# Two more up units per layer with seven products, two plain ones fewer, and the first unit's preparation reordered

## The chip, the cores and the metric

One core of one Trainium2 chip runs the whole program in one launch. The metric is the device time in microseconds (us). Engines: TensorE (PE, with its weight loads PEld), VectorE (DVE), ScalarE (ACT), GpSimd (POOL), and SyncE (SP), which issues the loads of the weights.

## The reference, cut to what matters

A decoder trunk of two layers over 512 tokens of width 1024, all in float32. Each layer is a token mixer, a cross-attention and a gated MLP, each between two RMS norms. The change is in the MLP's up projection:

```
def conv_ffn(h, w_up, conv_w, conv_b, w_down):
    u = h @ w_up                      # (512, 1024) @ (1024, 5632)
    a, b = u[..., :D_FF], u[..., D_FF:]        # D_FF = 2816
    a = causal_depthwise_conv(a, conv_w, width 3) + conv_b
    return (gelu(a) * b) @ w_down
```

## The kernel before, in words

**Products of three.** Every float32 operand is split into a high and a low fp32r part, and a product is three matmuls (`three`, L2161 to L2165): low by high, high by low, high by high. The high part of a weight is a copy by ACT, the low part a subtraction by POOL.

**Units.** The weights come in 70 units per layer of at most 1 MB, through a ring of two buffers `raw`, `w_hi` and `w_lo` (even units in slot 0, odd ones in slot 1). Units 36 to 57 are the up projection: for each of 11 pairs a unit of 256 value columns (even) and one of 256 gate columns (odd). SP loads a unit once the unit two before it has been turned into its low parts.

**Plain units.** A plain unit of the up projection is 2 column tiles x 8 blocks of k x 3 = 48 matmuls of 512 columns (`cols_gemm`). Units 36 and 37 do the same by halves of the tokens, as 256-column matmuls, in buffers of their own (`up_hi`, `up_lo`). The last plain unit has a loop of its own, with k outermost, which gives its places in the ring back in four steps (`part_spent`).

**Units with seven products.** From `U_SEVEN` on, `SEVENS` units are computed by the Winograd form of Strassen's scheme. Tokens (2 x 256), k (2 x 512) and columns (2 x 128) are cut in two each, and seven products of half-sized blocks take the place of eight: 7 x 4 x 3 = 84 matmuls of 256 columns. In the order in which PE issues them, with the bank that they add to: "11" (c11), "s2" (c21), "s1" (c12), "12" (c11), "s3" (c21), "s4" (c12), and "22" (c21), which `product_4` issues behind the "11" of the next unit. Within a unit:

- On the weights' side DVE makes four sums `s1`, `s2`, `s3`, `s4` (`part_sum`). `s2` and the unit's quarter 21 stand in upper halves of PSUM banks, where ACT copies the quarter (`copy_21`, place `psum_21`). ACT makes the high parts (`part_high`, order `HI_PARTS`: 11, s1, s2, 12, s4, s3), POOL the low parts (`part_low`, order `LO_PARTS`: 11, s1, 12, s3, s4), and DVE that of s2 (`part_s2_low`). The low part of s1 overwrites the sum s1, so POOL waits with it until s2 is made.
- The parts lie in eight places of the ring (`place_of`, `HELD`); `wait_place` waits until the place's last user is done.
- Between products, ACT copies c11 after "11" (`keep_first`, signal `kept_1`), DVE adds it to c21 and c12 (`keep_sixth`, `keep_fifth`), and `make_22`, `make_12`, `make_21` finish the four quarters. "12" may be issued only after `kept_1`, "s3" only after `kept_16`, "s4" only after `kept_15`.

**Token sums.** The tokens' side needs four sums of quarters of the activations, once per layer, `tok_sum[0..3]`, each with a high part (ACT, `token_high(i)`) and a low part. DVE makes sums 0, 1 and 3 (`token_sum`), POOL makes sum 2, the "third token sum" (`token_sum_3`, three passes), and its low part (`token_low_3`, needed by product "s3"). DVE makes the other low parts. `token_high(3)` and its low part write over a quarter of `a_hi` and `a_lo`, so they wait for the last plain unit. They are used by product "22".

**Behind the products** DVE does the convolution's taps (`conv_taps`) and the gating (`gate`), and ACT the gelu (`gelu_of`), for each column tile f of 22. For the plain pairs f = 0 to 5, for the others f = 6 to 21, whose first tap ACT does (`tap`).

**Order.** Every engine executes one list written out by hand, in order; only semaphores tie them together. The lists around the start of the seven-product units are in the ACT block (from `token_high(0)`), the DVE block (from `token_sum(0)`), the POOL block (the loop over u) and the PE block (behind the loop over units 36 and 37).

Of the kernel before, what the change touches and what calls it, by code (L numbers as in the profile page):

```python
# [48 lines left out]
UNITS = 70  # L49


U_SEVEN, SEVENS = 42, 16
PLAIN = 3
HELD = 8
assert UNITS % RING == 0
IN_W = [512] * 5 + [280]
# [207 lines left out]
def build(nc, x, mem, positions, norm_mix_pre, norm_mix_post, w_in, w_out, cmp_pe_k, cmp_pe_v,  # L264
# [4 lines left out]
    with ctx:  # L269
# [369 lines left out]

        def psum_21(w):  # L640

            return banks[:, 1024 * (2 * (w % 2) if w else 3):][:, 0:1024].rearrange("p (i n) -> p i n", i=2)[:, :, 256:512]

        def psum_s2(w):

# [261 lines left out]
        def _(pool):  # L907
# [26 lines left out]
            for l in range(DEPTH):  # L934
# [90 lines left out]
                    inc(pool.tensor_tensor(part_of(w_lo, w, "22"), quarter(U_SEVEN + w, 1, 1), part_of(w_hi, w, "22").bitcast(F32), ALU.subtract), part_22_lo)  # L1025

                for u in range(UNITS):
                    if u == U_SEVEN - 2:
                        token_sum_3()
                    if u == U_SEVEN:  # L1030
                        token_low_3()
                        for w in range(SEVENS):
                            part_low(w, "11")
                            if w:
                                part_22_low(w - 1)
                            for part in LO_PARTS[1:]:
                                part_low(w, part)
                        part_22_low(SEVENS - 1)
                    if U_SEVEN <= u < U_SEVEN + SEVENS:
                        continue  # L1040
                    if u == U_OUT + RING:
                        xk_rest()
                    if u == U_XO + 1:
                        for i in range(16):
                            xscale(i)
                    if u == U_XK:
                        for half in range(LO_STEPS.count(-1)):
                            low_half(U_XK, half)
                        for i in range(NI + 1):
                            if i == 0:  # L1050
                                pool.wait_ge(qk.sem, qk.at(l, 1))
                                inc(pool.memset(vc_tiles[:], 0.0), vc_cleared)
                            if i < NI and KIND[i] == "sb":
                                stick_relu(i)
                            if i + 1 < NI and KIND[i + 1] == "cmp":
                                cmp_shift(i + 1)
                            if i >= 2 and KIND[i - 2] == "cmp":
                                cmp_scale(i - 2)
                            if i and SOFT[i - 1]:
                                pool_scale(i - 1)  # L1060
                            if i and KIND[i - 1] == "sb":
                                stick_log(i - 1)
                            if i in O_LO_STEPS:
                                o_rest(O_LO_STEPS[i])
                            if i in LO_STEPS:
                                low_half(U_XK + LO_STEPS.index(i) // 2, LO_STEPS.index(i) % 2)
                    if U_XK <= u < U_OUT + RING:
                        continue
                    if l == 0 and u < 2:
                        pool.wait_ge(hi_made.sem, hi_made.at(0, 2 * u + 2))  # L1070
                        part_lo, part, part_hi = (v(u, 1) for v in (lo_half, raw_half, hi_half))
                        pool.tensor_tensor(part_lo[:, 0], part[:, 0], part_hi[:, 0].bitcast(F32), ALU.subtract).then_inc(pro_third, 1)
                        pool.wait_ge(pro_low, 2 + u)
                        inc(pool.tensor_tensor(part_lo[:, 1], part[:, 1], part_hi[:, 1].bitcast(F32), ALU.subtract), lo_made, 2)
                        continue
                    if u == in_unit(4, 1):
                        pool.wait_ge(first_low.sem, first_low.at(l, 1))
                        low_half(u, 1, 2)
                        continue
                    if u == U_UP + 1:  # L1080
                        pool.wait_ge(rows_done.sem, rows_done.at(l, T + 2))
                    for half in range(2):
                        low_half(u, half)
# [3 lines left out]
        def _(act):  # L1087
# [28 lines left out]
            for l in range(DEPTH):  # L1116
# [21 lines left out]
                def cast_to(n):  # L1138

                    cast_halves(2 * n)  # L1140
# [337 lines left out]
                def copy_21(w):  # L1478

                    u = U_SEVEN + w  # L1480
                    act.wait_ge(raw_landed[u % RING], landed(l, u))
                    if w == 0:
                        act.wait_ge(gT_done.sem, gT_done.at(l, 4))
                    elif w == 1:
                        act.wait_ge(gT_done.sem, gT_done.at(l, 6))
                    else:
                        done = (conved, gT_done)[w % 2]
                        act.wait_ge(done.sem, done.at(l, column(w - 2, 0) + 1))
                    inc(act.activation(k_of(psum_21(w)), by_halves(quarter(u, 0, 1)), ACT.Copy), copied_21)
# [9 lines left out]
                gelu_of(0)  # L1499
                token_high(1)  # L1500
                gelu_of(1)
                cast_to(U_UP + 5)
                token_high(2)
                gelu_of(2)
                gelu_of(3)
                cast_to(U_UP + 6)
                copy_21(0)
                for part in HI_PARTS[:4]:
                    part_high(0, part)
                gelu_of(4)  # L1510
                gelu_of(5)
                for part in HI_PARTS[4:]:
                    part_high(0, part)
                token_high(3)
                for w in range(SEVENS):
                    after_value, more = w % 2 == 1, w + 1 < SEVENS
                    if after_value:
                        tap(w - 1, 0)
                    keep_first(w)
                    part_high(w, "22")  # L1520
                    if more:
                        part_high(w + 1, "11")
                    if after_value:
                        tap(w - 1, 1)
                    elif w:
                        gelu_of(column(w - 1, 1))
                    if more:
                        copy_21(w + 1)
                        for part in ("s1", "s2", "12"):
                            part_high(w + 1, part)  # L1530
                    if after_value:
                        gelu_of(column(w, 0))
                    if more:
                        part_high(w + 1, "s4")
                        part_high(w + 1, "s3")
                    if w in (8, 10, 12):
                        g_parts((w - 8) // 2)
                gelu_of(NF - 1)
                cast_to(U_DOWN + 1)
                act.preload_act_table_set("natural_log_exp_and_others")  # L1540
# [22 lines left out]
        def _(dve):  # L1563
# [59 lines left out]
            for l in range(DEPTH):  # L1623
# [392 lines left out]
                def part_sum(w, part):  # L2016
# [8 lines left out]
                        ins = dve.tensor_tensor(by_halves(dst), by_halves(quarter(u, 1, 0)), k_of(psum_s2(w)), ALU.subtract)  # L2025
                    elif part == "s2":
                        dve.wait_ge(part_summed.sem, part_summed.at(l, nth(SUMS, w, "s1")))
                        if w >= 2 and w % 2 == 0:
                            dve.wait_ge(tapped.sem, tapped.at(l, w))
                        ins = dve.tensor_tensor(k_of(dst), by_halves(s1), by_halves(quarter(u, 0, 0)), ALU.subtract)  # L2030
# [48 lines left out]
                conv_taps(1)  # L2079
                gate(0)  # L2080
                gate(1)
                token_sum(3)
                token_low(0)
                conv_taps(2)
                token_low(1)
                conv_taps(3)
                gate(2)
                gate(3)
                conv_taps(4)
                part_sum(0, "s1")  # L2090
                part_sum(0, "s2")
                conv_taps(5)
                part_sum(0, "s3")
                part_sum(0, "s4")
                part_s2_low(0)
                gate(4)
                gate(5)
                for w in range(SEVENS):
                    if w:
                        make_12(w - 1)  # L2100
                        columns(w - 1, 0)
                        if w in (10, 12, 14):
                            g_rest((w - 10) // 2)
                        make_21(w - 1)
                    if w == 0:
                        dve.wait_ge(tok_hi_made.sem, tok_hi_made.at(l, 4))
# [44 lines left out]
        def _(pe):  # L2151
# [28 lines left out]
            for l in range(DEPTH):  # L2180
# [557 lines left out]
                                inc(ins, (up_psum, unit_used)[m])  # L2738

                cols_gemm(U_UP + 2, up_bank(1, 0), up_psum)  # L2740
                cols_gemm(U_UP + 3, up_bank(1, 1), up_psum)
                pe.wait_ge(gT_done.sem, gT_done.at(l, 2))
                cols_gemm(U_UP + 4, up_bank(2, 0), up_psum)
                hi, lo = unit(U_SEVEN - 1)
                for k in range(KD):
                    if k == 4:
                        rest(U_SEVEN - 1)
                    for m in range(2):
                        mm = slice(P * m, P * m + P)
                        ins = three(bank(up_bank(2, 1) + m), hi[:, k, mm], lo[:, k, mm], a_hi[:, k, :], a_lo[:, k, :], k == 0, k == KD - 1)  # L2750
                        if k == KD - 1:
                            inc(ins, (up_psum, unit_used)[m])
                    if k in (1, 3, 5):
# [18 lines left out]
                def wait_banks(w, name):  # L2772

                    if w < 2:
                        done, n = (conved, gT_done)[w], {"c11": 5, "c12": 6, "c21": 3}[name]
                    else:
                        done, n = (conved, gT_done)[w % 2], column(w - 2, name == "c21") + 1
                    pe.wait_ge(done.sem, done.at(l, n))
# [64 lines left out]
```

## Time and profile before

| | us |
|---|---|
| median of 3 runs (1657.83 to 1657.98) | 1657.86 |
| the profiled execution's own time | 1657.59 |
| its span, first to last instruction | 1655.9 |
| PE busy in the span | 1642.2 (99%) |
| DVE / ACT / POOL busy | 838.5 / 846.6 / 968.3 |
| mean granted TensorE clock | 0.999 |

Times in rows are microseconds from the start of the span. The columns of the stretch in the last group are PE, PEld, DVE, ACT, POOL, granted clock, DMA share and GB/s. In a timeline the first number is the start, the second the duration, behind them the engine, line, operation, output<-inputs, shape and count. An idle time before it, if there is any, is in brackets with what ended it. Durations of matmuls overlap: their pace is read from start to start. The first layer's up projection lies from 477 to 708 us.

### The profile page before, as it was taken

The page shows a single profiled execution, that of the slowest core. Times are in us where ns is not written, and L with a number is a line of the kernel's source. Part 1 is how long each engine was busy: PE and PEld are TensorE (multiplying, and loading weights), DVE is VectorE, ACT ScalarE, POOL GpSimd, SP SyncE. Part 2 cuts the span into 40 slices and gives each one's busy share as a digit, 9 for nine tenths or more (in the row PEclk, how much of TensorE's full clock was granted, in tenths as well). Part 3 has the DMA queues.
Part 4 walks back from the last instruction along what each step waited for, and adds up shares of the span by engine and source line. Part 5 has one row for each costly group of instructions (what it writes and reads, how often), then busy time and mean ns, then how long its engine had stood idle before and what let it go on. Part 6 is the DMA issues. An engine that isn't in the chain of part 4 may idle for free.

```text
span 1655.9 us, 26967 instructions
## 1 busy us (share of the span) xinstructions
PE 1642.2 (99%) x10369; PEld 1401.6 (85%) x10369; DVE 838.5 (51%) x1733; ACT 846.6 (51%) x1650; POOL 968.3 (58%) x689
## 2 busy tenths in 40 slices
PE   9999999999999999999999999999999999999998
PEld 7888766888888999988888887768888989999886
DVE  3454676072368677721243456652532877777113
ACT  6326777263463566532362367763643636566222
POOL 4456668464338777755624467674634387776552
PEclk9999999999999999999999999999999999999999
DMA  6224111143123233332323340112422223332421
GB/s 231 77 94 142 52 27 52 64 141 102 64 77 102 77 103 103 103 127 102 112 94 94 101 142 27 27 52 89 141 76 68 81 94 102 103 103 83 139 85 76
DMA packets 101210, 154.39 MB, mean 93 GB/s; under 512 B 4396, under 2 KB 76380, under 8 KB 101084
## 3 DMA queue, kind: packets, MB, share of 16 engines
q1 hardware_dynamic: 98572, 147.16, 27.3%
q10 hardware_dynamic: 2512, 5.51, 1.0%
q8 instruction: 84, 1.38, 0.4%
q14 instruction: 42, 0.34, 0.1%
HBM read 150.56 MB, written 2.10 MB: 92 GB/s over the span
## 4 chain that ended last, share of the span: by engine, by line
PE 95%; ACT 1%; issue 1%; DVE 1%; POOL 1%; DVEq 0%; ACTq 0%; POOLq 0%
PE banks L2163 27%; PE banks L2165 26%; PE banks L2164 26%; PE banks L2478 4%; PE banks L2531 4%; PE banks L2507 4%; PE banks L2291 1%; PE banks L2207 1%; DVE proj L1851 1%; PE banks L2527 0%; PE banks L2675 0%; PE banks L2195 0%; POOL w_lo L938 0%; ACT w_hi L1135 0%; ACT rows L1098 0%
## 5 line engine op out<-in xcount | busy, mean ns | idle before, releaser
L938 POOL TENSOR_TENSOR w_lo<-raw,w_hi 128x1024 fp32r<-128x1024 f32 (+2 forms) x198 | 486.2, 2475 | 422.6 <-ACT w_hi L1135 409.8
L1135 ACT ACTIVATE w_hi<-raw 128x1024 fp32r<-128x1024 f32 (+2 forms) x200 | 195.5, 1020 | 328.9 <-PE banks L2165 321.2
L2163 PE MATMUL banks<-w_hi,a_lo 128*128 128x512 f32 (+1 forms) x864 | 332.5, 385 | 0.1
L2165 PE MATMUL banks<-w_hi,a_hi 128*128 128x512 f32 (+1 forms) x864 | 330.1, 382 | 0.0
L2164 PE MATMUL banks<-w_lo,a_hi 128*128 128x512 f32 (+1 forms) x864 | 330.0, 382 | 0.0
L2163 PE MATMUL banks<-a_hi,w_lo 128*128 128x256 f32 (+1 forms) x768 | 245.2, 319 | 0.0
L2165 PE MATMUL banks<-a_hi,w_hi 128*128 128x256 f32 (+1 forms) x768 | 244.6, 318 | 0.0
L2164 PE MATMUL banks<-a_lo,w_hi 128*128 128x256 f32 (+1 forms) x768 | 244.5, 318 | 0.0
L2163 PEld LDWEIGHTS banks<-w_hi,a_lo 128*128 128x128 f32 x864 | 162.3, 188 | 32.8 <-issue 1.7
L2165 PEld LDWEIGHTS banks<-w_hi,a_hi 128*128 128x128 f32 x864 | 162.2, 188 | 31.5
L2164 PEld LDWEIGHTS banks<-w_lo,a_hi 128*128 128x128 f32 x864 | 162.3, 188 | 30.3
L2165 PEld LDWEIGHTS banks<-a_hi,w_hi 128*128 128x128 f32 x768 | 146.4, 191 | 10.1
L2164 PEld LDWEIGHTS banks<-a_lo,w_hi 128*128 128x128 f32 x768 | 146.4, 191 | 9.7
L2163 PEld LDWEIGHTS banks<-a_hi,w_lo 128*128 128x128 f32 x768 | 146.2, 190 | 9.5
L1020 POOL TENSOR_TENSOR w_lo<-w_sum,w_hi 128x512 fp32r<-128x512 f32 x64 | 83.0, 1296 | 56.5 <-DVE banks L2030 40.9
L2164 PE MATMUL banks<-tok_lo,w_hi 128*128 128x256 f32 x384 | 108.8, 283 | 0.0
L2163 PE MATMUL banks<-tok_hi,w_lo 128*128 128x256 f32 x384 | 108.7, 283 | 0.0
L2165 PE MATMUL banks<-tok_hi,w_hi 128*128 128x256 f32 x384 | 108.3, 282 | 0.0
L1962 DVE TENSOR_TENSOR a_lo<-gT,a_hi 128x1024 fp32r<-128x1024 f32 x18 | 28.7, 1593 | 153.7 <-ACT a_hi L1435 153.7
L1020 POOL TENSOR_TENSOR w_lo<-raw,w_hi 128x512 fp32r<-128x512 f32 x64 | 84.8, 1324 | 25.9 <-ACT w_hi L1468 25.9
L1837 DVE CUSTOM_DVE_ANT_0 banks<-banks,causal 128x128 f32<-128x128 f32 (+3 forms) x160 | 75.6, 512 | 40.2 <-PE banks L2478 40.2
L948 POOL TENSOR_SCALAR proj<-proj,rden,gates 128x128 f32<-128x128 f32 (+3 forms) x128 | 76.4, 609 | 22.9 <-DVE rden L1855 22.5
(321 smaller groups left out, 3461.8 us busy)
## 6 DMA issues: line engine op xcount, KB each, us to landing
raw<-in_ffn_w_up SPq DMA_DIRECT2D x44, 1024.0 KB, 5.1
raw<-in_ffn_w_down SPq DMA_DIRECT2D x20, 1024.0 KB, 4.8
raw<-in_w_in SPq DMA_DIRECT2D x19, 1024.0 KB, 5.0
raw<-in_x_wk SPq DMA_DIRECT2D x8, 1024.0 KB, 5.5
raw<-in_x_wv SPq DMA_DIRECT2D x8, 1024.0 KB, 4.9
raw<-in_x_wq SPq DMA_DIRECT2D x8, 1024.0 KB, 5.2
raw<-in_x_wo SPq DMA_DIRECT2D x8, 1024.0 KB, 4.9
raw<-in_cmp_wk SPq DMA_DIRECT2D x4, 1024.0 KB, 5.2
```

The source lines that it names most:

```text
L938: inc(pool.tensor_tensor(lo_half(u, half), raw_half(u, half), hi_half(u, half).bitcast(F32), ALU.subtract), lo_made, n)
L948: inc(pool.tensor_scalar(p, p, r, gate_of(i, hp), ALU.mult, ALU.mult), scaled_pool)
L1020: inc(pool.tensor_tensor(lo, src, hi.bitcast(F32), ALU.subtract), piece_lo)
L1135: inc(act.activation(hi_half(u, half), raw_half(u, half), ACT.Copy), hi_made)
L1837: inc(dve.tensor_tensor_reduce(x, x, causal[:, S - n:S], -1.0, 3.0e38, ALU.add, ALU.min, stat(neg_max, i, hp)), maxed)
L1962: inc(dve.tensor_tensor(part_lo, gT[:, k[0]:k[-1] + 1, :], part_hi.bitcast(F32), ALU.subtract), g_lo)
L2163: pe.matmul(dst, st_lo, mv_hi, start=first, stop=False, skip_group_check=shared)
L2164: pe.matmul(dst, st_hi, mv_lo, start=False, stop=False, skip_group_check=shared)
L2165: return pe.matmul(dst, st_hi, mv_hi, start=False, stop=last, skip_group_check=shared)
L2478: ins = pe.matmul(s_bank(i, hp, n + extra, key_at(i) - extra), qT[half, m, P * t:P * t + P], keys(row, n, extra)[half], start=True, stop=True)
L2507: ins = pe.transpose(bank(4 + hp, P, P * k), probs(i, hp)[:, P * k:P * k + P], ident[:])
L2531: ins = pe.matmul(bank(6, P, P * t)[half], proj[:, k, col:col + HD], pT(i)[:, kg, P * k:P * k + P], start=kind != "win" and t == 0 and k = ...
```

## The change

`PLAIN` goes from 3 pairs to 2, `U_SEVEN` from 42 to 40 and `SEVENS` from 16 to 18. So in each layer units 40 and 41 are computed with seven products; units 36 to 39 stay plain, and 39 takes over the loop that frees its places step by step. The lists of ACT and DVE around the start are rearranged. In POOL's list the third token sum stands where it stood, behind the low halves of unit 39; what stood behind it (the low halves of units 40 and 41) is gone, and the low part of the third sum moves from ahead of the first unit's parts to between its "12" and its "s3". Quarter 21 of the first unit goes to banks 4 and 5 in place of 6 and 7. The steps that make the first parts of the down projection's input keep their distance from the end.

```
-U_SEVEN, SEVENS = 42, 16
-PLAIN = 3
+U_SEVEN, SEVENS = 40, 18
+PLAIN = 2
 def psum_21(w):
-    banks[:, 1024 * (2 * (w % 2) if w else 3):] ...
+    banks[:, 1024 * (2 * (w % 2) if w else 2):] ...
# POOL
-    if u == U_SEVEN - 2:
+    if u == U_SEVEN:
         token_sum_3()
-    if u == U_SEVEN:
-        token_low_3()
         for w in range(SEVENS):
             part_low(w, "11")
             if w:
                 part_22_low(w - 1)
             for part in LO_PARTS[1:]:
+                if w == 0 and part == "s3":
+                    token_low_3()
                 part_low(w, part)
# ACT, copy_21
-    if w == 0:
-        act.wait_ge(gT_done.sem, gT_done.at(l, 4))
-    elif w == 1:
-        act.wait_ge(gT_done.sem, gT_done.at(l, 6))
+    if w < 2:
+        act.wait_ge(gT_done.sem, gT_done.at(l, 2))
# ACT, list
 gelu_of(1)
-cast_to(U_UP + 5)
 token_high(2)
+copy_21(0)
+for part in HI_PARTS[:2]:
+    part_high(0, part)
 gelu_of(2)
+for part in HI_PARTS[2:4]:
+    part_high(0, part)
 gelu_of(3)
-cast_to(U_UP + 6)
-copy_21(0)
-for part in HI_PARTS[:4]:
-    part_high(0, part)
-gelu_of(4)
-gelu_of(5)
 for part in HI_PARTS[4:]:
     part_high(0, part)
 token_high(3)
...
-    if w in (8, 10, 12):
-        g_parts((w - 8) // 2)
+    if w in (10, 12, 14):
+        g_parts((w - 10) // 2)
# DVE, part_sum "s2"
+    if w == 0:
+        dve.wait_ge(conved.sem, conved.at(l, 4))
# DVE, list
 gate(0)
 gate(1)
-token_sum(3)
 token_low(0)
+token_low(1)
+part_sum(0, "s1")
 conv_taps(2)
-token_low(1)
 conv_taps(3)
-gate(2)
-gate(3)
-conv_taps(4)
-part_sum(0, "s1")
 part_sum(0, "s2")
-conv_taps(5)
 part_sum(0, "s3")
 part_sum(0, "s4")
 part_s2_low(0)
-gate(4)
-gate(5)
+token_sum(3)
+gate(2)
+gate(3)
 for w in range(SEVENS):
...
-    if w in (10, 12, 14):
-        g_rest((w - 10) // 2)
+    if w in (12, 14, 16):
+        g_rest((w - 12) // 2)
# PE
 cols_gemm(U_UP + 2, up_bank(1, 0), up_psum)
-cols_gemm(U_UP + 3, up_bank(1, 1), up_psum)
-pe.wait_ge(gT_done.sem, gT_done.at(l, 2))
-cols_gemm(U_UP + 4, up_bank(2, 0), up_psum)
 ...                        # the loop of unit U_SEVEN - 1, now into up_bank(1, 1)
-    if w < 2: done, n = (conved, gT_done)[w], {"c11": 5, "c12": 6, "c21": 3}[name]
+    if w < 2: done, n = (conved, gT_done)[w], {"c11": 1, "c12": 2, "c21": 3}[name]
```

## Rows read from the trace of the kernel before

**Rows 1.** Part 1 of the page: busy time of each engine.

```profile
PE 1642.2 (99%) x10369; PEld 1401.6 (85%) x10369; DVE 838.5 (51%) x1733; ACT 846.6 (51%) x1650; POOL 968.3 (58%) x689
```

**Rows 2.** Waits of PE over the span: us in total, times, longest.

```profile
PE banks L2163 <- ACT xkT L1318: 3.8, 4, 1.0
PE banks L2155 <- POOL ident L915: 2.5, 1, 2.5
```

**Rows 3.** PE's timeline: unit 38's first matmul, then first ones of products.

```profile
503.34 0.40 PE L2163 MATMUL banks<-a_hi,w_lo 128*128 128x512 f32 x1
...
546.87 0.28 PE L2163 MATMUL banks<-a_hi,w_lo 128*128 128x256 f32 x1
...
567.02 0.28 PE L2163 MATMUL banks<-a_hi,w_lo 128*128 128x256 f32 x1
```

**Rows 4.** POOL's timeline from 507 us, the end of the plain units.

```profile
507.90 3.38 POOL L997 TENSOR_TENSOR tok_sum<-a_hi 128x1024 f32<-128x1024 f32 x1
511.24 2.40 POOL L998 TENSOR_TENSOR tok_spare<-a_lo 128x1024 f32<-128x1024 f32 x1
513.72 3.27 POOL L1000 TENSOR_TENSOR tok_sum<-tok_sum,tok_spare 128x1024 f32<-128x1024 f32 x1
...
533.49 2.40 POOL L1005 TENSOR_TENSOR tok_lo<-tok_sum,tok_hi 128x1024 fp32r<-128x1024 f32 x1
...
538.72 1.29 POOL L1020 TENSOR_TENSOR w_lo<-w_sum,w_hi 128x512 fp32r<-128x512 f32 x1
...
551.25 1.30 POOL L1025 TENSOR_TENSOR w_lo<-raw,w_hi 128x512 fp32r<-128x512 f32 x1
```

**Rows 5.** DVE's timeline in the same stretch, and one row of the second layer.

```profile
512.04 0.69 DVE L1969 TENSOR_TENSOR gT<-gel,banks 128x512 f32<-128x512 f32 x1 [0.20 <-ACT gel L1442]
512.65 2.08 DVE L2008 TENSOR_TENSOR tok_sum<-a_hi,tok_sum 128x1024 f32<-128x1024 f32 x1
514.76 3.31 DVE L2009 TENSOR_TENSOR tok_sum<-tok_sum,a_lo 128x1024 f32<-128x1024 f32 x1
...
523.55 1.22 DVE L2014 TENSOR_TENSOR tok_lo<-tok_sum,tok_hi 128x1024 fp32r<-128x1024 f32 x1
...
537.52 0.74 DVE L1985 TENSOR_SCALAR conv<-banks,vecs 128x512 f32<-128x512 f32 x1
...
539.75 0.68 DVE L2035 TENSOR_TENSOR w_sum<-raw,banks 128x512 f32<-128x512 f32 x1
540.35 0.68 DVE L2025 TENSOR_TENSOR s_sum<-raw,banks 128x512 f32<-128x512 f32 x1
...
553.03 0.68 DVE L2035 TENSOR_TENSOR w_sum<-raw,banks 128x512 f32<-128x512 f32 x1
...
1333.65 2.08 DVE L2008 TENSOR_TENSOR tok_sum<-a_hi,tok_sum 128x1024 f32<-128x1024 f32 x1
```

**Rows 6.** ACT's timeline in the same stretch.

```profile
517.02 1.06 ACT L1453 ACTIVATE tok_hi<-tok_sum 128x1024 fp32r<-128x1024 f32 x1 [0.52 <-POOL tok_sum L1000]
...
529.56 0.58 ACT L1489 ACTIVATE banks<-raw 128x512 f32<-128x512 f32 x1
...
536.91 0.63 ACT L1468 ACTIVATE w_hi<-w_sum 128x512 fp32r<-128x512 f32 x1
...
547.13 1.06 ACT L1453 ACTIVATE a_hi<-tok_sum 128x1024 fp32r<-128x1024 f32 x1 [4.29 <-PE banks L2165]
548.50 0.38 ACT L1476 ACTIVATE keep<-banks 128x256 f32<-128x256 f32 x1 [0.31 <-PE banks L2165]
...
557.43 1.15 ACT L1468 ACTIVATE w_hi<-raw 128x512 fp32r<-128x512 f32 x2
```

**Rows 7.** SP's timeline and its DMAs' time to landing: the load of unit 44.

```profile
552.63 0.37 SPq L889 DMA_DIRECT2D raw<-in_ffn_w_up  x1
...
DMA to landing us min/median/max: 5.0/5.1/5.3
```

**Rows 8.** A stretch of the steady seven-product units: its length, then busy time of each engine.

```profile
568.00:690.00 122.00, 122.00 (x1019) 122.00 (x1018) 89.22 (x159) 76.37 (x138) 92.46 (x74) 1.00 0.32 105
```

More of the change, by code:

```diff
@@ L640, in psum_21 @@
         def psum_21(w):
-            return banks[:, 1024 * (2 * (w % 2) if w else 3):][:, 0:1024].rearrange("p (i n) -> p i n", i=2)[:, :, 256:512]
+            return banks[:, 1024 * (2 * (w % 2) if w else 2):][:, 0:1024].rearrange("p (i n) -> p i n", i=2)[:, :, 256:512]
         def psum_s2(w):
@@ L2749, in _ @@
                         mm = slice(P * m, P * m + P)
-                        ins = three(bank(up_bank(2, 1) + m), hi[:, k, mm], lo[:, k, mm], a_hi[:, k, :], a_lo[:, k, :], k == 0, k == KD - 1)
+                        ins = three(bank(up_bank(1, 1) + m), hi[:, k, mm], lo[:, k, mm], a_hi[:, k, :], a_lo[:, k, :], k == 0, k == KD - 1)
                         if k == KD - 1:
@@ L2774, in wait_banks @@
                     if w < 2:
-                        done, n = (conved, gT_done)[w], {"c11": 5, "c12": 6, "c21": 3}[name]
+                        done, n = (conved, gT_done)[w], {"c11": 1, "c12": 2, "c21": 3}[name]
                     else:
```

## The prediction

> **What bounds the kernel.** I read the page's busy times first: PE is busy for 1642.2 of 1655.9 us, the next engine, POOL, for 968.3 [rows 1]. The reader should see that only two things can move the time: the number and width of PE's matmuls, and holes in PE's stream. The list of PE's waits says how few holes there are: 6.3 us in the whole span, and none in the up projection [rows 2]. So the change is worth what it takes off PE's stream, less the holes that it tears. PE's timeline gives the price of either kind of unit [rows 3], and the timelines of POOL, DVE and ACT between 507 and 558 us [rows 4 to 6] give what is needed to lay the new lists out by hand. The second layer shows the same at 821.0 us later (DVE's L2008 of 2.08 us at 512.65 comes again at 1333.65 [rows 5]), so one layer is worked out and counted twice.
>
> **What PE saves.** From 503.34 to 546.87 lie the 192 matmuls of the four plain units 38 to 41, back to back: 43.53 / 4 = 10.88 us a unit. From 546.87 to 567.02 lie 14 products: 1.44 us each, 10.08 us for the seven of a unit [rows 3]. So one conversion saves 0.80 us, not the eighth that the count of columns promises (1.36), because a 256-column matmul takes 120 ns, more than half of the 227 ns of a 512-column one. Two units in two layers: 4 x 0.80 = **3.2 us saved** if PE never waits. That is 0.19% of the time.
>
> **What is late.** What prepares the first seven-product unit (w = 0) now has until the end of unit 39, at 503.34 + 2 x 10.88 = 525.1, where it had until 546.87. The two plain units that went away were the cover for the token sums. The steps up to `gate(1)` are untouched (DVE ends them at 512.7 [rows 5]). I lay out the rest:
>
> - POOL and DVE get in each other's way. POOL's L998 ends at 513.64; DVE's L2008, issued at 512.65, takes 2.08 where its like takes 1.22 alone (523.55), and ends at 514.73. POOL's L1000, issued at 513.72, then takes 3.27 instead of 2.40 and ends at 516.99; DVE's L2009, issued at 514.76, takes 3.31 and ends at 518.07 [rows 4, 5]. So they take turns: about 1.1 us for DVE, 2.26 for POOL, and whoever waits goes next. A DVE operation with a PSUM input doesn't take part (0.68 to 0.75 us).
> - DVE's `token_low(0)` and `token_low(1)` are operations of the same shape in the place of those two, so they end at 514.7 and 518.07. ACT's `token_high(2)` still starts at 517.02, behind POOL's third sum, and ends at 518.08 [rows 6]; `copy_21(0)` now stands behind it and ends at 518.56 (0.58).
> - DVE: s1 518.66 to 519.34, the taps of f = 2 and 3 (3 x 0.78 each, after 537.52 [rows 5]) to 523.8, s2 to 524.5, s3 to 525.1 (each 0.68 or a little more). PE's "11" waits for s3 and starts at about 525.2: a hole of 0.1 us. ACT makes the high part of s2 by 525.17, of "12" by 525.69; DVE makes s4 by 525.93 and the low part of s2 by 526.54, just in time for "s2" at 526.64.
> - POOL can make the low part of s1 only after s2: 524.6 to 525.9 (1.29 [rows 4]); that of "12" 525.9 to 527.15; and then, newly in this place, `token_low_3`.
> - DVE comes to `token_sum(3)` at 526.45, two SBUF passes. The first waits for POOL's "12" and runs 527.15 to 528.25. POOL's `token_low_3`, waiting since 527.15, takes 528.25 to 530.5. The second pass depends on the first and so cannot have got in ahead of it; it runs 530.5 to 531.6.
> - ACT stands in `token_high(3)` until then: 531.65 to 532.7 (1.06). Queued behind it is `keep_first(0)`, 532.6 to 533.0 (0.38 [rows 6]). That copy of c11 was free to go since 526.7, but PE's "12", due at 525.2 + 3 x 1.44 = 529.5, waits for it. **Hole: 3.5 us.** In the kernel before, `token_high(3)` began at 547.13 and the copy was made at 548.9, against a "12" due at 551.2.
> - Behind that, "s3" is due at 534.5 and needs `keep_sixth(0)`, which stands in DVE's list behind `gate(2)`, `gate(3)` and the low part of token sum 3. These gates end at 532.8; POOL ends the low part of s3 in the same 0.1 us. If DVE goes first, `keep_sixth` is done at 534.3: no hole. If POOL does, 1.1 us later: a hole of 1.05.
> - The next units inherit lateness. s3 of w = 1, which had 1.8 us in hand (made at 553.71, product due at 555.50 [rows 5]), is made at 537.6 against 537.4 (another 0.2, or 0.4 in POOL's case). SP loads unit w = 2 once POOL has the low part "22" of w = 0, which came 2.9 us ahead of the second unit's first product (552.55 [rows 4]; the issue is at 552.63, landing takes 5.1 [rows 7]) and now comes 0.5 behind it. ACT's copy of the new unit, the second operation at 557.43, had just 0.1 to 0.3 us in hand [rows 6], so it slips by 3.3 us; s3 of w = 2 had 2.0 in hand and costs perhaps 0.25. After that the preparation catches up, since DVE and POOL are idle for a quarter of the steady stretch (89.22 and 92.46 of 122 us busy [rows 8]).
>
> Sum of a layer: 0.1 + 3.5 + 0 + 0.2 + 0.25 = 4.05 if DVE wins the tie, 0.1 + 3.5 + 1.05 + 0.4 = 5.05 if POOL does. Neither order is favoured by a row, so I take the middle, **4.5 us a layer**, 9.0 for two. Net 9.0 - 3.2 = +5.8.
>
> **What is taken at nothing.** The added unit's work on DVE, ACT and POOL lies under its 10.08 us of PE, as in the steady stretch, where no engine but PE is busy for more than 76% [rows 8]. The end of the up projection moves as a whole: g_parts, g_rest and the cast of unit 58 keep their distance to the last product; cover gone, each would open a hole of its own in the down projection. The wait on `conved` 4 is on DVE's own last operation, 0.04 us. The other bank of quarter 21 changes nothing in length.
>
> **A rule beside the turns.** The rows show POOL and DVE taking turns by whole instructions, 3.3 us for a pair [rows 4, 5]. The Trainium skill (SBUF — State Buffer, Who interferes with whom) says that DVE with two SBUF inputs and GpSimd exclude each other for a whole instruction, and that the order of issue decides; by that, the trace agrees. It speaks against this change: it puts `token_sum(3)` and `token_low_3` at one moment, with ACT and PE behind the loser. Without the rule, with both at full speed, the hole would be 0.7 us.
>
> **Rivals.**
>
> 1. *No turns.* `token_sum(3)` finds the port free or wins both times: 526.45 to 528.75, the copy of c11 at 530.15, a hole of 0.7. A layer costs 0.1 + 0.7 + at most 0.2: 1.0. Net 2.0 - 3.2 = -1.2: 1656.7. For it: the margins are tenths (POOL's "12" would have to be over by 526.45, not 527.15). Against it: three collisions in a row went the other way.
> 2. *No hole at all.* Faster: all steps run 0.8 us earlier than I lay them, for instance if POOL's third sum, which now sees the same two collisions, ended early. It decides from `kept_1` at 529.5, and then gives the whole 3.2: 1654.7, which at 0.19% is still just inside of no change. The other side of 0.2% needs 0.1 us more than the arithmetic has.
> 3. *Late weights.* The load of w = 2 and then of w = 3 slips more than the next units catch up. If ACT's 3.3 us are not absorbed, because `keep_fifth` stands behind the s1 of the next unit, each of the next two units opens about 1 us: 6.5 us a layer, net +9.8: 1667.7. For it: 0.1 us in hand at 557.97. Against it: the next load has 1.6 us in hand again.
> 4. *The clock.* The granted clock is 1.0 wherever PE waits in this trace, but no wait is over 1.0 us behind the start [rows 2]. If a hole of 3.5 us took it from 2.4 to 1.2 GHz, each product at that level would take 1.44 us more; two of them in each layer give +5.8: 1669.5. The Trainium skill (TensorE: Matmul & The Clock Gate, What's actually happening) describes such a fall after idling; no row here shows it.
>
> **How the numbers follow.** Chances: my forecast 0.50, rival 1 0.20, rival 2 0.10, rival 3 0.13, rival 4 0.07. The time: 1657.86 + 5.8 = **1663.7** (the profiled execution, at 1657.59, would come to 1663.4). 0.2%, about what a measurement of this kernel can tell from no change, is 3.3 us, so the limits are 1654.5 and 1661.2. Slower: the forecast, 3 and 4, less the part of the forecast in which a hole is a microsecond shorter: 0.64. Within 0.2%: rivals 1 and 2 and that part: 0.32. Faster by more: 0.04. The range leaves out rival 4, half of rival 2 and the far end of 3: **1655.5 to 1667.0**. The forecast's own range is 1662.8 to 1664.8.
>
> **What would show it.** Units 38 and 39 at 10.88 us, w = 0 starting at about 525.2. In PE's waits, a new one of 3.5 us, twice, on ACT's `keep_first` (the operation keep<-banks), with `token_high(3)` right ahead of it on ACT and DVE's tok_sum<-tok_sum,a_lo, 3.3 us long, ahead of that. Perhaps 1 us on keep<-banks,keep of DVE. Steady units of 10.08 us from w = 3 on. I am wrong if DVE's two passes for the fourth token sum take 1.2 us each, if "12" starts before 531, or if the clock drops below 1.0 there.

## The result, and the profile after

| | before | changed |
|---|---|---|
| median of 4 runs, us | 1657.86 | 1667.36 |
| lowest to highest | 1657.83 to 1657.98 | 1666.39 to 1668.57 |
| ratio, with its 95% interval | | 1.0058 (1.0040 to 1.0075) |
| the profiled execution: its time, its span | 1657.59, 1655.9 | 1668.25, 1666.5 |

The changed kernel is slower by 9.5 us, 0.57%. Slower was forecast, by 5.8; the time lies 0.36 us above the stated range. The four runs come in two pairs, 1666.39 and 1666.46, which lie inside the range, and 1668.25 and 1668.57; the profile is of the run of 1668.25. Part 1 of the page of the changed kernel, against [rows 1]: PE has 144 matmuls more (336 of 256 columns in place of 192 of 512) and gains 2.8 us of busy time in a span that is 10.6 longer.

```profile
PE 1645.0 (99%) x10513; PEld 1410.9 (85%) x10513; DVE 859.0 (52%) x1769; ACT 859.6 (52%) x1682; POOL 982.1 (59%) x705
```

The list of PE's waits in the changed kernel, which answers to [rows 2], names the forecast hole: twice, on ACT's `keep_first` (L1476), 3.3 us each. (The list counts from the end of the matmul before; counted by how much later than due the product starts, as the prediction does, it is 3.5.) Two short ones are new as well.

```profile
PE banks L2157 <- ACT keep L1476: 6.7, 2, 3.3
PE banks L2157 <- ACT xkT L1318: 3.9, 4, 1.0
PE banks L2149 <- POOL ident L915: 2.5, 1, 2.5
PE banks L2157 <- issue: 0.5, 1, 0.5
PE banks L2157 <- DVE w_sum L2033: 0.4, 1, 0.4
```

PE's timeline of the changed kernel in the first layer, against [rows 3]: unit 38's first matmul, the first of "11", of "12" and of "s3" of the first seven-product unit.

```profile
503.43 0.40 PE L2157 MATMUL banks<-a_hi,w_lo 128*128 128x512 f32 x1
...
525.79 0.35 PE L2157 MATMUL banks<-a_hi,w_lo 128*128 128x256 f32 x1 [0.41 <-DVE w_sum L2033]
...
533.68 0.42 PE L2157 MATMUL banks<-a_hi,w_lo 128*128 128x256 f32 x1 [3.34 <-ACT keep L1476]
...
536.24 0.41 PE L2157 MATMUL banks<-tok_hi,w_lo 128*128 128x256 f32 x1
```

From "12" to "s3" pass 2.56 us where a product takes 1.44. What lies in there is seen in the stretches of the same kernel (columns as in [rows 8]; the last but two is the granted clock), in the first layer and in the second.

```profile
528.00:530.00 2.00, 2.00 (x19) 2.00 (x18) 1.97 (x2) 0.00 (x0) 2.00 (x1) 1.00 0.00 0
530.00:532.00 2.00, 0.34 (x3) 0.14 (x2) 2.00 (x1) 0.00 (x0) 2.00 (x2) 1.00 0.00 0
532.00:534.00 2.00, 0.32 (x2) 0.35 (x3) 2.00 (x4) 1.80 (x4) 2.00 (x2) 0.96 0.00 0
534.00:536.00 2.00, 2.00 (x11) 2.00 (x11) 2.00 (x3) 1.06 (x3) 1.89 (x2) 0.50 0.00 0
536.00:538.00 2.00, 2.00 (x15) 2.00 (x14) 2.00 (x3) 0.63 (x1) 2.00 (x2) 0.69 0.00 0
...
1360.00:1362.00 2.00, 1.46 (x7) 1.20 (x7) 2.00 (x5) 0.53 (x1) 2.00 (x2) 0.50 0.00 0
1362.00:1364.00 2.00, 2.00 (x11) 2.00 (x11) 2.00 (x2) 0.63 (x3) 1.30 (x2) 0.50 0.00 1
1364.00:1366.00 2.00, 2.00 (x12) 2.00 (x11) 1.65 (x4) 1.70 (x4) 2.00 (x2) 0.50 0.86 288
```

PE idles from 530.3 to 533.7, and behind that the clock is granted at half, 1.2 GHz, for 3 to 4 us in the first layer and for some 7 in the second. An engine that reads "busy 2.00 of 2.00" with 11 matmuls in place of 19 is the sign, since PE's starts are then 213 ns apart in place of 120 ("12" to "s3": 2.56 us for 12 matmuls).

DVE's timeline of the changed kernel, against [rows 5], shows the chain that makes the hole: `token_low` 0 and 1 (5.42 together), s2 (L2028) and s3 (L2033), the two passes of token sum 3, the gates, its low part (L2101) and `keep_sixth` (L2045).

```profile
512.74 5.42 DVE L2010 TENSOR_TENSOR tok_lo<-tok_sum,tok_hi 128x1024 fp32r<-128x1024 f32 x2
...
524.36 0.70 DVE L2028 TENSOR_TENSOR banks<-w_sum,raw 128x512 f32<-128x512 f32 x1 [0.46 <-DVE conv L1983]
524.97 0.68 DVE L2033 TENSOR_TENSOR w_sum<-raw,banks 128x512 f32<-128x512 f32 x1
...
526.93 1.92 DVE L2004 TENSOR_TENSOR tok_sum<-a_hi,tok_sum 128x1024 f32<-128x1024 f32 x1
528.88 3.29 DVE L2005 TENSOR_TENSOR tok_sum<-tok_sum,a_lo 128x1024 f32<-128x1024 f32 x1
532.09 1.27 DVE L1965 TENSOR_TENSOR gT<-gel,banks 128x512 f32<-128x512 f32 x2
533.29 2.33 DVE L2101 TENSOR_TENSOR a_lo<-tok_sum,a_hi 128x1024 fp32r<-128x1024 f32 x1
535.54 0.41 DVE L2045 TENSOR_TENSOR keep<-banks,keep 128x256 f32<-128x256 f32 x1
```

ACT's timeline, against [rows 6]: idle for 4.33 us in front of `token_high(3)`, with the copy of c11 queued behind it.

```profile
532.20 1.06 ACT L1453 ACTIVATE a_hi<-tok_sum 128x1024 fp32r<-128x1024 f32 x1 [4.33 <-DVE tok_sum L2005]
533.16 0.37 ACT L1476 ACTIVATE keep<-banks 128x256 f32<-128x256 f32 x1
```

POOL's timeline, against [rows 4]: the low part of "12", that of token sum 3 between DVE's two passes, that of s3 behind the second.

```profile
526.45 1.32 POOL L1020 TENSOR_TENSOR w_lo<-raw,w_hi 128x512 fp32r<-128x512 f32 x1
527.71 3.37 POOL L1005 TENSOR_TENSOR tok_lo<-tok_sum,tok_hi 128x1024 fp32r<-128x1024 f32 x1
531.05 2.25 POOL L1020 TENSOR_TENSOR w_lo<-w_sum,w_hi 128x512 fp32r<-128x512 f32 x1
```

**Where the 10.6 us of the profiled spans are.** From unit 38's first matmul to the first one of the down projection the kernel before took 204.80 us in either layer. The changed kernel took 208.90 and 210.47: less the 1.60 saved, holes and clock cost 5.70 and 7.27. Another 0.3 lies ahead of the two stretches, and 0.6 behind the second, where the last stores take 2.5 us to land in place of 2.0.

### The profile page after: what moved, and what is told of

Read it like the earlier page. It is cut to its first block, busy times and chain, and to the rows that moved or that the text cites. A ratio compares the mean times of both kernels' runs of the same rounds, so it can differ in the third digit from the quotient of the medians.

```text
span 1666.5 us, 27429 instructions
## 1 busy us (share of the span) xinstructions
PE 1645.0 (99%) x10513; PEld 1410.9 (85%) x10513; DVE 859.0 (52%) x1769; ACT 859.6 (52%) x1682; POOL 982.1 (59%) x705
## 4 chain that ended last, share of the span: by engine, by line
PE 91%; POOL 3%; DVE 2%; ACT 2%; issue 1%; DVEq 0%; ACTq 0%; POOLq 0%
PE banks L2157 25%; PE banks L2158 25%; PE banks L2159 25%; PE banks L2472 4%; PE banks L2525 4%; PE banks L2501 4%; POOL w_lo L938 2%; PE banks L2285 1%; PE banks L2201 1%; DVE proj L1847 1%; PE banks L2521 0%; PE banks L2669 0%; ACT w_hi L1135 0%; PE banks L2189 0%; POOL tok_sum L997 0%
## 5 line engine op out<-in xcount | busy, mean ns | idle before, releaser
L938 POOL TENSOR_TENSOR w_lo<-raw,w_hi 128x1024 fp32r<-128x1024 f32 (+2 forms) x190 | 463.6, 2459 | 412.3 <-ACT w_hi L1135 399.6
L1135 ACT ACTIVATE w_hi<-raw 128x1024 fp32r<-128x1024 f32 (+2 forms) x192 | 187.5, 1018 | 323.7 <-PE banks L2159 316.2
L2157 PE MATMUL banks<-a_hi,w_lo 128*128 128x256 f32 (+1 forms) x768 | 239.9, 312 | 7.1 <-ACT keep L1476 6.7
L2158 PE MATMUL banks<-a_lo,w_hi 128*128 128x256 f32 (+1 forms) x768 | 239.0, 311 | 0.0
L2159 PE MATMUL banks<-a_hi,w_hi 128*128 128x256 f32 (+1 forms) x768 | 239.0, 311 | 0.0
L1020 POOL TENSOR_TENSOR w_lo<-w_sum,w_hi 128x512 fp32r<-128x512 f32 x72 | 95.5, 1326 | 68.3 <-DVE banks L2028 55.3
L2157 PE MATMUL banks<-tok_hi,w_lo 128*128 128x256 f32 x432 | 123.2, 285 | 0.5 <-issue 0.5
L2158 PE MATMUL banks<-tok_lo,w_hi 128*128 128x256 f32 x432 | 123.1, 285 | 0.0
L2159 PE MATMUL banks<-tok_hi,w_hi 128*128 128x256 f32 x432 | 122.5, 284 | 0.0
L1020 POOL TENSOR_TENSOR w_lo<-raw,w_hi 128x512 fp32r<-128x512 f32 x72 | 96.1, 1335 | 21.4 <-ACT w_hi L1468 21.2
```

The source lines that it names most:

```text
L938: inc(pool.tensor_tensor(lo_half(u, half), raw_half(u, half), hi_half(u, half).bitcast(F32), ALU.subtract), lo_made, n)
L1020: inc(pool.tensor_tensor(lo, src, hi.bitcast(F32), ALU.subtract), piece_lo)
L1135: inc(act.activation(hi_half(u, half), raw_half(u, half), ACT.Copy), hi_made)
L2157: pe.matmul(dst, st_lo, mv_hi, start=first, stop=False, skip_group_check=shared)
L2158: pe.matmul(dst, st_hi, mv_lo, start=False, stop=False, skip_group_check=shared)
L2159: return pe.matmul(dst, st_hi, mv_hi, start=False, stop=last, skip_group_check=shared)
```

## The experiments

All times are medians; the kernel before came to 1657.8 beside each of them, and each is an edit of the changed kernel.

| | median (lowest to highest), us | ratio to before (95%) |
|---|---|---|
| e1: low part of the third sum in front | 1662.53 (1661.91 to 1663.72) | 1.0029 (1.0017 to 1.0041) |
| e2: copy of c11 ahead of `token_high(3)` | 1668.72 (1668.20 to 1669.69) | 1.0065 (1.0048 to 1.0081) |
| e3: hole filled with repeated matmuls | 1665.97 (1665.97 to 1665.98) | 1.0049 (1.0034 to 1.0064) |
| e4: e1 and e2, and DVE's keeps earlier | 1662.13 (1661.95 to 1662.40) | 1.0026 (1.0016 to 1.0036) |
| e5: e4, and first passes of the taps on ACT | 1660.20 (1660.02 to 1660.38) | 1.0014 (1.0005 to 1.0023) |
| e6: only the first passes on ACT | 1662.84 (1662.43 to 1663.23) | 1.0030 (1.0019 to 1.0041) |
| e7: e5, DVE's list put right again | 1656.71 (1655.90 to 1656.96) | 0.9992 (0.9983 to 1.0001) |

**e1.** POOL's low part of token sum 3 moves; nothing else.

```
 token_sum_3()
+token_low_3()
 for w in range(SEVENS):
...
-    if w == 0 and part == "s3":
-        token_low_3()
```

> Only GpSimd's low part of the third token sum moves, back in front of the first unit's parts, where GpSimd stands idle for 5 us. Theory (GpSimd and VectorE take turns on a port by whole instructions): the second pass of token_sum(3) no longer waits for a 2.26 us instruction but for one of 1.2, so it ends about 1.0 us earlier in each layer and the hole ahead of the product 12 shrinks from 3.5 to about 2.5 us. With a granted clock that stays at 1.0 that gives 1662 to 1663; if the clock falls for holes of 2.5 us too, 1664 to 1665.5. Rival (VectorE's own list sets the end of that sum, whatever GpSimd does): hole 3.5, time 1666 to 1668 as changed.

Measured: the new kernel's row in PE's waits, DVE's second pass in its timeline, and two stretches with the granted clock.

```profile
PE banks L2156 <- ACT keep L1475: 4.5, 2, 2.2
```

```profile
528.68 2.19 DVE L2004 TENSOR_TENSOR tok_sum<-tok_sum,a_lo 128x1024 f32<-128x1024 f32 x1
```

```profile
532.00:536.00 4.00, 3.62 (x22) 3.65 (x23) 3.69 (x6) 2.40 (x5) 2.53 (x3) 0.73 0.00 0
1356.00:1360.00 4.00, 3.99 (x21) 4.00 (x22) 3.69 (x6) 2.03 (x4) 2.52 (x2) 0.57 0.00 0
```

The second pass takes 2.19 us where it took 3.29, and the hole shrinks by the same 1.1. So the length of POOL's instruction sets how long DVE waits, and the rival falls. The time went down by 4.8 us, more than 1.1 for each layer: behind the earlier pass DVE's low part of token sum 3 met no instruction of POOL (1.23 us long, as alone, where it had taken 2.33), so what it adds to the lateness of "s3" went too. The clock fell behind the holes of 2.2 us in this execution as well, but for a shorter time: 0.73 and 0.57 are means over 4 us that are part at half, part at full clock.

```profile
532.00 1.23 DVE L2100 TENSOR_TENSOR a_lo<-tok_sum,a_hi 128x1024 fp32r<-128x1024 f32 x1
```

It did not fall as far in every run. Three of the six have a mean granted clock of 0.999 over the whole span, as the kernel before has, and take 1661.91 to 1662.10 us; the other three have 0.998 or 0.997 and take 1662.96 to 1663.72, the profiled one longest.

**e2.** One ACT instruction moves.

```
 for part in HI_PARTS[4:]:
     part_high(0, part)
+keep_first(0)
 token_high(3)
 for w in range(SEVENS):
-    keep_first(w)
+    if w:
+        keep_first(w)
```

> Only ScalarE's copy of c11 (keep_first of the first unit) moves ahead of token_high(3). Theory (VectorE's list is late as a whole): the hole ahead of the product 12 is gone, and one of about 4.3 us opens one product later, ahead of s3, which waits for keep_sixth behind the gates and the low part of token sum 3 on VectorE. Time within 1 us of the changed kernel's 1667.4. Rival (the copy queued behind token_high(3) is the whole trouble): both holes gone, 1658 to 1660.

Measured: PE's timeline at "s3" of the first unit, and the clock behind it.

```profile
536.14 0.55 PE L2159 MATMUL banks<-tok_hi,w_lo 128*128 128x256 f32 x1 [4.28 <-issue]
```

```profile
536.00:540.00 4.00, 3.86 (x18) 3.89 (x19) 3.86 (x7) 1.75 (x3) 3.30 (x3) 0.50 0.16 34
```

"12" starts on time, at 530.26, and "s3" 4.3 us late: the hole moved by one product, as expected, and the time is 1.4 us above the changed kernel's, a little outside the 1 us. The rival, both holes gone, is out. The hole before "12" was only the first of the waits that DVE's lateness can take. The view names no releaser for this wait ("issue"), but DVE's `keep_sixth`, which "s3" needs, ends 0.1 us ahead of it:

```profile
535.63 0.41 DVE L2047 TENSOR_TENSOR keep<-banks,keep 128x256 f32<-128x256 f32 x1
```

**e3.** The product s1 of the first unit is issued three times, so that PE has work in the hole. The last one clears the bank again, so nothing is added up twice.

```
+if w == 0:
+    for _ in range(2):
+        repeat(w, "s1", "c12", tok_hi[0], tok_lo[0], True)     # the 12 matmuls, no signal
 product(w, "s1", "c12", tok_hi[0], tok_lo[0], True)
```

> The product s1 of the first unit is issued three times in place of once, each time from a cleared bank: 24 matmuls more, 2.88 us, which lie in the hole of 3.5 us. Theory (the granted clock falls because TensorE idles there, and costs about 3 us): clock 1.0 through both starts, time 1664.3 (1663.5 to 1665), and the runs within 0.4 us of one another. Rival (the clock plays no part in the time, the preparation alone sets it): unchanged, 1666.4 to 1668.6. Second rival (the falls come from elsewhere): clock still falls, time 1667 or more.

Measured: PE's timeline at the starts of "12", "s3" and the second unit's "11", and the stretches of the first layer.

```profile
533.68 0.36 PE L2157 MATMUL banks<-a_hi,w_lo 128*128 128x256 f32 x1 [0.47 <-ACT keep L1476]
...
536.09 0.36 PE L2157 MATMUL banks<-tok_hi,w_lo 128*128 128x256 f32 x1 [0.75 <-issue]
...
539.34 0.36 PE L2157 MATMUL banks<-a_hi,w_lo 128*128 128x256 f32 x1 [0.15 <-DVE w_sum L2033]
```

```profile
528.00:532.00 4.00, 4.00 (x36) 4.00 (x35) 3.96 (x2) 0.00 (x0) 4.00 (x2) 1.00 0.00 0
532.00:536.00 4.00, 2.87 (x23) 2.49 (x21) 4.00 (x6) 2.86 (x5) 3.92 (x3) 1.00 0.00 0
536.00:540.00 4.00, 3.76 (x29) 3.62 (x30) 3.86 (x6) 1.75 (x3) 3.30 (x3) 1.00 0.13 36
```

The clock stays at 1.0, and the four runs, which lay 2.2 us apart in the changed kernel, lie within 0.01. So the fall of the clock comes from the idle time, and with it the scatter of this kernel. But it is worth 1.4 us in the medians, not 3: the time lies above the theory's 1663.5 to 1665 and below the first rival's 1666.4. With the clock at 1.0 a second hole shows ahead of "s3" (2.41 us from start to start, 0.97 too many) and a third ahead of the second unit's "11" (0.31 too many), which the half-speed matmuls of the changed kernel had covered in the first layer. There the two spans from unit 38 to the down projection are nearly the same, 208.79 against 208.90; in the second layer they are 208.43 against 210.47.

**e4.** Three moves together, to take the waiting instructions from behind one another. The cuts of e4, e5 and e7 give the steps in short.

```
# POOL as in e1.  ACT:
+keep_first(0); part_high(0, "22"); part_high(1, "11"); copy_21(1)
 token_high(3)
# DVE, between the two passes of token_sum(3):
+keep_sixth(0); keep_fifth(0)
# DVE, w = 0: the low part of token sum 3 goes from the front to behind s3 of the next unit
 part_sum(1, "s1"); part_sum(1, "s2"); part_sum(1, "s3")
+tok_lo[3] = tok_sum[3] - tok_hi[3]
 part_sum(1, "s4"); make_22(0); part_s2_low(1)
```

> Three moves together: GpSimd's low part of the third sum in front again; VectorE makes keep_sixth and keep_fifth of the first unit between the two passes of token_sum(3), and the low part of token sum 3 only after the second unit's s3; ScalarE makes c11's copy, the parts 22 and 11 and the copy of quarter 21 ahead of token_high(3). Theory: no hole ahead of 12, s3 and s4; s3 of the second unit is made about 535.5 against a product due at 534.5, so a hole of 0.6 at the start and of 1 to 1.5 us ahead of the second unit's 11 stay in each layer, the clock stays at 1.0, and the time is 1658 to 1659.5. Rival (the stretch holds more work than VectorE and GpSimd can do in it, and the hole only moves again): a hole of over 3 us somewhere in the first two units, 1664 or more.

Measured: PE's waits.

```profile
PE banks L2166 <- DVE w_sum L2040: 3.2, 3, 1.4
...
PE banks L2166 <- DVE banks L2063: 2.3, 2, 1.2
```

The holes ahead of "12" and "s3" are gone and the clock stays at 1.0. In their place stand 1.5 us ahead of the second unit's "11" (its s3, as expected; 1.4 in the list) and 1.4 ahead of the first unit's "22" (1.2 in the list), which waits for `make_22` behind the low part of token sum 3 on DVE. That second one was not expected: 1662.1 in place of 1658 to 1659.5. The rival, one hole of over 3 us, did not come either.

**e5.** In addition ACT, idle ahead of `token_high(2)`, does the first of three convolution passes for f = 2 and 3.

```
# ACT, behind gelu_of(1)
+for f in (2, 3):
+    wait_cols(act, l, up_psum, 2, U_UP + 2, f - 2)
+    if f == 3: act.wait_ge(gelued.sem, gelued.at(l, 1))
+    act.activation(conv[:, f % 3, 0:S], bank(...), ACT.Copy, scale=wcol(2))
# DVE, conv_taps: that pass only for f < 2, else a wait for ACT's
```

> The kernel of the three moves (e4), and ScalarE makes the first of the three passes of the convolution for the column tiles 2 and 3 of the last plain pair, in time that it spends idle in front of token_high(2); VectorE's list becomes 1.5 us shorter ahead of the first unit's s2. Theory (VectorE's work between 512.7 and 536 us is what is late, and every us taken off it there comes off the holes): the start hole of 0.6 goes, of the two holes of 1.5 and 1.4 us ahead of the second unit's 11 and the first unit's 22 at most 1.5 together stays in each layer, clock 1.0, time 1655.5 to 1657.5, below the kernel before. Rival (GpSimd, with its low parts one behind the other, is late by then, or the copies on ScalarE): holes of over 2 us in a layer stay, 1659 or more.

Measured: 1660.20, above the theory's 1655.5 to 1657.5. The start hole is gone (525.23), and the two others are 1.1 and 1.4 us, 2.5 in a layer, so the size is the rival's (over 2 us, 1659 or more). Its cause is not: DVE's timeline shows that with e4's order DVE now waits for PE between the passes, so the time taken off its list comes back in part as idle time of 1.43 and 0.96 us.

```profile
525.02 1.92 DVE L2018 TENSOR_TENSOR tok_sum<-a_hi,tok_sum 128x1024 f32<-128x1024 f32 x1
528.36 0.42 DVE L2061 TENSOR_TENSOR keep<-banks,keep 128x256 f32<-128x256 f32 x1 [1.43 <-PE banks L2177]
529.74 0.42 DVE L2066 TENSOR_TENSOR keep<-banks,keep 128x256 f32<-128x256 f32 x1 [0.96 <-PE banks L2177]
530.09 1.59 DVE L2021 TENSOR_TENSOR tok_sum<-tok_sum,a_lo 128x1024 f32<-128x1024 f32 x1
```

**e6.** The changed kernel with only e5's edit.

> The changed kernel with nothing but ScalarE's first passes for the column tiles 2 and 3: token_high(3), the copy of c11 and GpSimd's low part of the third sum stay where the change put them. Theory (the hole ahead of 12 is set by the end of VectorE's two passes for token sum 3): that end comes earlier by 1.2 to 1.5 us, the hole shrinks to 2.0 to 2.6 us less what the earlier start of the unit (0.5) gives back, time 1663 to 1664.5. Rival (the turns with GpSimd alone set that end, since GpSimd's low part of s1 waits for VectorE's s2 and moves with it): the end moves by the full 1.5 only if both move together; if it doesn't move at all, 1666 or more.

Measured: 1662.84. The holes ahead of "12" are 2.1 us, and the second pass, 3.31 us long, ends at 530.33, 1.8 earlier: POOL's low parts of s1 and "12" stand behind s2 and moved with it, and so did the collision. Since both lists moved together, this run fits the theory and the rival alike and does not decide between them; it shows that an earlier end of the passes is an earlier "12". The end moved by more than the expected 1.2 to 1.5, and the time is 0.2 below what was expected. The clock falls here too. PE's wait, DVE's second pass and the stretch behind the hole:

```profile
PE banks L2166 <- ACT keep L1477: 4.2, 2, 2.1
```

```profile
527.02 3.31 DVE L2014 TENSOR_TENSOR tok_sum<-tok_sum,a_lo 128x1024 f32<-128x1024 f32 x1
```

```profile
532.00:536.00 4.00, 3.69 (x20) 3.42 (x21) 4.00 (x5) 1.86 (x4) 3.90 (x3) 0.61 0.00 0
```

**e7.** DVE's list once more, from e5.

```
-token_sum(3, (keep_sixth, keep_fifth))
+token_sum(3)
 gate(2); gate(3)
 # w = 0
+keep_sixth(0); part_sum(1, "s1"); keep_fifth(0); part_sum(1, "s2"); part_sum(1, "s3")
+make_22(0)
+tok_lo[3] = tok_sum[3] - tok_hi[3]
 part_sum(1, "s4"); part_s2_low(1)
```

> The kernel with ScalarE's first passes (e5), with VectorE's list put right once more, by the trace of e5, where VectorE stood idle for 2.4 us between the two passes of token_sum(3): both passes run one behind the other again, then the gates, keep_sixth, s1, keep_fifth, s2, s3 of the second unit, make_22 of the first, and only then the low part of token sum 3, s4 and the low part of s2. Theory (the holes are only a matter of where each step stands in VectorE's list, there is now room for all of it): pass two ends at about 529.2, keep_sixth at 530.7 against a product due at 531.0, s3 of the second unit at 533.0 against 533.9, no hole over 0.3 us is left in either layer, the saved 3.2 us show but for the 0.5 us that the last store took longer in all kernels so far: 1655.1 (1654.7 to 1656.0). Rival (VectorE and GpSimd are full there in sum, so that a hole moves to the product 22, which waits for the low part of token sum 3): 1 us or more stays in each layer, 1657 or more.

Measured: 1656.71. PE's waits have lost the hole, and the longest new wait is 0.3 us; from unit 38 to the down projection the two layers take 203.97 and 204.03 us, 0.8 less than before, with 0.8 of the 1.60 still given back at the second unit's "11" and the first unit's "22".

```profile
PE banks L2175 <- ACT xkT L1318: 3.8, 4, 1.0
PE banks L2167 <- POOL ident L916: 2.5, 1, 2.5
PE banks L2175 <- DVE a_lo L2129: 0.5, 2, 0.3
```

All eleven runs of it (1655.90 to 1656.96) lie below all fifteen runs of the kernel before beside it (1657.52 to 1658.01), but the interval of the ratio reaches 1.0001, so a gain of 1 us is seen and not secured. It was expected at 1655.1 (1654.7 to 1656.0), the rival at 1657 or more, with 1 us or more left in each layer: the median lies between the two, and the small holes at the two products, 0.8 in a layer, make up the 1.6 us over the expectation. The eleven runs lie 1.06 us apart although all of them have a mean clock of 0.999, so a scatter of this size need not come from the clock.

## Why the prediction was right or wrong, point by point

**What PE saves: right.** Units at 10.88 and 10.08 us, 0.80 each; in the changed kernel products are 1.44 us apart wherever the clock is full and nothing waits.

**The layout of the lists: right, to some tenths, up to the hole.** DVE's lows ended at 518.16 (forecast 518.07), s3 at 525.65 (525.1), the second pass of token sum 3 at 532.17 (531.6), the copy of c11 at 533.53 (533.0), and the hole was 3.5 us (3.5). From s2 on all are 0.5 late in the first layer, since DVE stood idle for 0.46 us ahead of s2, behind the last tap of the convolution, where the prediction took 0.04 for the wait on DVE's own `conved`. The start hole was 0.60. In the second layer the same wait stands in the same place, s2 starts 0.10 us behind the end of the tap, and the start hole was 0.18. So the wait alone does not cost 0.46; what else did is open.

```profile
1348.39 0.75 DVE L1983 SCALAR_TENSOR_TENSOR conv<-banks,vecs,conv 128x510 f32<-128x510 f32 x1
1349.24 0.70 DVE L2028 TENSOR_TENSOR banks<-w_sum,raw 128x512 f32<-128x512 f32 x1
```

**The turns on the port: right.** e1 took POOL's long instruction from between the passes, and 1.1 us of the hole went. The Trainium skill (SBUF — State Buffer, Who interferes with whom) has a VectorE instruction with two SBUF inputs contend with a GpSimd one that reads SBUF, with the order of issue deciding which of them blocks. The collisions shown here fit it, DVE's two passes at 1.92 and 3.29 us against 1.22 alone among them; e1 shows that POOL's long instruction costs the hole 1.1 of its 3.5 us.

**The tie at 532.8: POOL won.** The low part of token sum 3 took 2.33 us, `keep_sixth` ended at 535.95, and e3 shows the hole that follows, 0.97 (forecast 1.05 for that case). The gates ended at 533.36, where POOL had gone on at 533.26, so it was decided by a tenth, and the forecast had no reason for either side. The middle of 0 and 1.05 had been taken. With the second unit's 0.31 (0.4) a layer comes, at full clock, to 5.59 and 5.23 us in e3 against the 4.5 of the sum and the 5.05 of its worse case.

**Late weights: no cost.** ACT waited 0.48 us for the load of the third unit and made that part at 543.28; no hole came of it. Rival 3 is out.

**The step that failed** is the clock, which the sum put at nothing. Rival 4 had a chance of 0.07, with the reason "The granted clock is 1.0 wherever PE waits in this trace, but no wait is over 1.0 us behind the start", and the range left it out. That reason carries nothing: with no row of a long hole the trace could not say what the clock does behind one, and the forecast itself put one of 3.5 us there. In the profiled execution the clock fell to half in both layers; the prediction had named that among its signs of being wrong. e3 keeps the clock at 1.0 and comes to 1665.97, inside the range, so this term decides on which side of the limit the time lies.

Its price had been put too high all the same: 5.8 us, against 1.4 in the medians of changed kernel and e3 (0.4 to 2.6 over the single runs, which come in two pairs, so that the 1.4 is the middle between them). A product at half speed took 2.56 us, 1.12 more and not 1.44, and part of what the slow matmuls cost they took from holes that followed.

The Trainium skill (TensorE: Matmul & The Clock Gate, What's actually happening) has two levels of the clock and the lower one after idling. The trace agrees: 0.50 behind the holes of 3.3 us, 1.00 ahead of them.

**The missing sum.** The time lies 3.7 us above the forecast of 5.8, and the clock is not the largest part of it. Forecast were 9.0 of holes; at full clock they were 10.8 (5.59 + 5.23). Of these 1.8 more, 1.1 is the tie, lost in both layers where half of it had been taken, and most of the rest the start holes (0.60 and 0.18 against 0.1). The clock added 1.4, and the last stores, which the prediction did not have in its sum, 0.5: 10.8 + 1.4 + 0.5 - 3.2 = 9.5 us, as measured. The sum closes, but the clock and the last stores are in it as differences of measured times and not worked out from causes. Rival 1 (no turns) is out. Rival 2 (no hole, 1654.7) is out for this order of the lists; e7, with ACT's two passes added and another order, comes to 1656.71 with 0.8 us of holes left in a layer.

**Left open.** Why the last stores land in 2.5 us in place of 2.0 in the changed kernel was not tried; they take 2.4 to 2.5 in all seven experiments too, so it does not hang on the holes or the clock. Nor was it tried how little idling lets the clock stay; the cases seen are below. Why e7's runs scatter, and what held s2 back in the first layer only, is open as well.

## What to carry to other kernels

A converted unit was worth 0.8 us and each hole at the start of the phase several times that: where a pipeline's warm-up loses its cover, lay out the lists of all engines around the new start before counting what the units save. Here a hole that was removed by moving the one instruction on its path came back at the next product (e2); look for the engine whose whole list is late and take work off that (e6), then read the trace again for its new idle time (e5, e7). And where a forecast puts a long idle stretch on TensorE into a trace that has none, the clock belongs in the sum, with its scatter.

## What the runs showed of the hardware that was not expected

In the profiled executions the granted clock fell to half behind single holes of 3.3 us (changed kernel), 2.2 us (e1), 2.1 us (e6) and 4.3 us (e2). Ahead of these holes PE had been busy but for 0.4 us at most in the last tens of us. It stayed at 1.0 behind pairs of holes of 1.4 and 1.2 us (e4), of 0.9 and 1.1 (e5), and of 0.5 and 0.8 (e3).

The fall is not the same in every run of a kernel, and it shows as scatter: the four runs of the changed kernel lie 2.2 us apart, those of e3 0.01. In e1 the mean granted clock of a run (0.997 to 0.999) goes with its time, from 1663.72 down to 1661.91 us. A look at the clock of every run tells more here than one profile does.

Where another engine is late anyway, half-speed matmuls are partly free: in the first layer of the changed kernel they cost 0.1 us net (208.90 against 208.79 in e3), in the second 2.0 (210.47 against 208.43).
